# The first quad's first row half of an expert layer, multiplied expert by expert with its row blocks in four column groups and folded afterwards

## The chip, the cores and the metric

One core of one Trainium2 chip. The metric is the time of one execution on the device, in microseconds (us). A core has five engines with queues of their own: TensorE (PE; its weight loads are PEld), VectorE (DVE), ScalarE (ACT), GpSimd (POOL) and SyncE (SP), which here only issues transfers; 16 DMA engines carry the transfers. SBUF is the on-chip memory, PSUM the accumulators of TensorE (eight banks of 128 x 512 fp32).

## What is computed

A decoder trunk of two layers on 256 tokens of width 1024, all in fp32. Layer 0 is a gated linear recurrence, layer 1 block-sparse attention; each is followed by a hierarchical mixture of 32 experts, which is what the change touches:

```python
def hier_moe(h, w_group, b_group, w_expert, b_expert, w_in, w_out):
    # top-1 group of 4, top-2 experts of the 8 in it, weights of each token
    ...
    def expert_block(args):
        xb, e = args
        hu = xb @ w_in[e]                                    # 1024 -> 2 x 512
        return (jax.nn.silu(hu[:, :EXPERT_FF]) * hu[:, EXPERT_FF:]) @ w_out[e]   # 512 -> 1024
    ...
```

Every expert's weights (4 MB for w_in, 2 MB for w_out) are read once per layer.

## The kernel before, in words

An expert layer goes through the 32 experts in 8 quads of 4 (QUADS, GRP). Each expert has room for 32 tokens (BLK), so a quad's tokens fill 128 rows. For a quad the tokens' features are gathered by products with a 0/1 matrix (`gather`, and for a layer's first quad `first_half` and `second_half`) into PSUM, scaled and copied to xgT, [128 features of block k, 4 experts x 32 tokens]. Then `up` multiplies: for a row block k of 128 rows of w_in, for the gate and for the up columns, four matmuls, one per expert, each with a stationary operand of 128x32 (the expert's tokens) and a moving one of 128x512 (the weights). The four write to different strips of 32 partitions of one bank, so they stand in the four column groups of the array. Eight row blocks make two row halves of four blocks each. Then come tanh (L699) and the products of silu (L1214, L1219), four transposes (`hidden_T`), `down` with w_out, and `combine`, which adds the result to the tokens' sums.

**Loads.** The weights come in slots of 2.097 MB (128 partitions x 16 KB): per quad, r = 12u to 12u+3 are the first row halves of its four experts, the next four the second row halves, the last four w_out. They go through a ring of 8 slots, all issued on the SP queue in a fixed order, each load waiting until the slot's last reader is done: `rows_done` (first row half of a quad multiplied), `up_done`, `down_done`. A layer's first loads are placed ahead of the layer; four of them (r = 0, 8, 9, 10) have homes outside the ring (EXTRA_HOME), r = 0 in the work regions 0 and 1.

**Around the change.** The loads r = 12, 13, 14 (first row halves of quad 1's experts) go to the slots of r = 1, 2, 3, which hold quad 0's first row halves of experts 1, 2, 3. Before, quad 0's first row half was multiplied block by block over all four experts. After block 0 and after block 1 TensorE signals `first_k_done`, and `load_freed` (L405 to L419, issue on L417) loads the same block, 0.5 MB, of the three new weights; after `rows_done` it loads blocks 2 and 3, 1 MB each: nine transfers. r = 15 to 18 (L372) wait for `up_done` of quad 0, r = 19 for its `down_done`, and r = 20 to 23 (w_out of quad 1) for `rows_done` and what follows in quad 1. DVE scales block 0 of the gathered tokens as soon as it is there (L965), blocks 1 to 3 after the gather (L967); ACT scales blocks 4 to 7 (`weighted_columns`, L638). Block 2's product stands behind half of the second gather, block 3's behind the other half. The counts per expert (two products with `ones`) follow, then the second row half (`up`, 64 records, since an fp32 matmul leaves two records) and the next quad's gather.

Of the kernel before, what the change touches and what calls it, by code (L numbers as in the profile page):

```python
# [15 lines left out]
ALU = mybir.AluOpType  # L16
# [3 lines left out]
P = 128  # L20
T = 256
TT = T // P
D = 1024
# [36 lines left out]
LATE = SMALL + 204 + 2 * KD * (NG + E) + NG + P  # L60
TAKEN = 1024
# [6 lines left out]
def build(nc, x, hg_w_in, hg_w_out, w_kv, att_w_q, att_w_o, rel_bias, moe_w_in, moe_w_out, c_turned, c_rows, c_first, c_late, c_masks, c_bucket, c_future, out):  # L68
    with ExitStack() as ctx:
# [14 lines left out]
        late = sb("late", [P, LATE])  # L84
# [16 lines left out]
        turn = late[:, LATE - P:LATE]  # L101
        ms = sb("ms", [P, 18])
# [60 lines left out]
        rt = region(5)  # L163
        wgt = rt[:, 384:448].rearrange("p (q a e) -> p q a e", a=TT, e=GRP)
# [52 lines left out]
        first_k_done = sem("first_row_blocks_done")  # L217
        first_k_gathered = sem("first_row_block_gathered")
        freed_in = [sem(f"freed_row_block{k}_in") for k in range(2)]
# [44 lines left out]
        def heads_bank(j, hp):  # L264

            return (4 + hp - 2) if j == 0 else (6 + hp) % 8

# [50 lines left out]
        def _(sp):  # L318
# [27 lines left out]
            def load_expert(layer, r, dst, src, it):  # L346
# [59 lines left out]
            def experts(layer):  # L406
                def load_freed(r0):
                    for part, ks in enumerate((slice(0, 1), slice(1, 2), slice(2, KD // 2))):
                        if part == 2:
                            sp.wait_ge(*expert_read(layer, 0, 0))  # L410
                        else:
                            sp.wait_ge(first_k_done, 2 * layer + part + 1)
                        for r in range(r0, r0 + GRP - 1):
                            c = ring_chunk(layer, r, 0)

                            def copy(dst, src):
                                sp.dma_start(dst[:, ks, :], src[:, ks, :])\  # L417
                                  .then_inc(loaded[c % RING] if part == 2 else freed_in[part], 16)

                            expert_chunk(layer, r % QC // GRP, GRP * (r // QC) + r % GRP, copy, chunk(c))  # L420

                def load_next(r, it):
                    if freed(r, it):
                        if r == RING + EXTRAS:
                            load_freed(r)
                        return
# [126 lines left out]
        def _(act):  # L553
# [107 lines left out]
            def moe(layer):  # L661
# [45 lines left out]

                act.wait_ge(gat_done, 2 * P0 + 2)
# [1316 lines left out]
```

## Time and profile before

| | |
|---|---|
| median of 3 runs | 1167.86 us (1167.62 to 1168.41) |
| the profiled execution | 1167.82 us, span 1166.0 us |
| TensorE busy | 866.5 us (74%) |
| VectorE, ScalarE, GpSimd busy | 269.6, 132.5, 24.0 us |
| moved | 447.76 MB, mean 384 GB/s |
| mean granted TensorE clock | 0.875 |

The page cuts the span into 40 slices of 29 us. In the lines of slices a digit is the busy share in tenths, and PEclk is the granted clock of TensorE in tenths of full speed. Slices 1 to 5 are the mixer of layer 0, 6 to 20 its experts, 21 to 25 the mixer of layer 1, the rest its experts. Times in the trace count from the start of the span.

### The profile page before, as it was taken

To read this page: it belongs to the slowest core of one execution; us is meant where nothing else is said; L and a number is where in the kernel's file an instruction comes from. 1 tells how busy PE (TensorE), PEld (TensorE's weight loads), DVE (VectorE), ACT (ScalarE), POOL (GpSimd) and SP (SyncE) were. 2 spreads that over 40 slices of the span, in tenths; PEclk is the share of its full clock that TensorE was granted. 3 is DMA by queue.
4 is the path that set the end of the run, shared out by engine and by line. 5 is a ranking of instruction groups with operands and counts; after the bars stand their busy time and mean duration, and the time that the engine had idled before them with its cause. 6 is when DMAs were issued, how large, how long until landed. Compare 5 with 4: busy or idle time off the path is not lost.

```text
span 1166.0 us, 12503 instructions
## 1 busy us (share of the span) xinstructions
PE 866.5 (74%) x5238; PEld 412.6 (35%) x5238; DVE 269.6 (23%) x504; ACT 132.5 (11%) x328; POOL 24.0 (2%) x27
## 2 busy tenths in 40 slices
PE   9999999946566655656689999986565656565666
PEld 7965655312121212222234565532222222222222
DVE  3565673010101010101038746301010101010102
ACT  2011211100000000000011241110000000000000
POOL 1000110000000000000002100000000000000000
PEclk9999999977878787878899999998788887877789
DMA  9985588999999999999999937899999999999997
GB/s 351 281 323 211 216 319 329 422 428 428 429 427 428 430 427 428 428 427 429 415 410 405 377 145 286 317 428 427 429 426 428 428 428 429 427 428 427 427 420 294
DMA packets 51817, 447.76 MB, mean 384 GB/s; under 512 B 4496, under 2 KB 6840, under 8 KB 26936
## 3 DMA queue, kind: packets, MB, share of 16 engines
q1 hardware_dynamic: 49696, 444.43, 92.1%
q10 hardware_dynamic: 2072, 2.62, 1.2%
q8 instruction: 38, 0.62, 0.2%
q14 instruction: 11, 0.09, 0.0%
HBM read 444.41 MB, written 2.62 MB: 383 GB/s over the span
## 4 chain that ended last, share of the span: by engine, by line
DMA 45%; PE 45%; SPq 5%; issue 2%; DVE 1%; ACT 1%; POOL 0%; DVEq 0%; POOLq 0%
PE ps L1394 44%; DMA ring<-in_moe_w_in 29%; DMA ring<-in_moe_w_out 15%; SPq L466 3%; SPq L372 2%; DMA ring<-in_w_kv 1%; PE ps L1397 1%; DMA xs<-const_turned 0%; ACT ps L668 0%; DVE work L1141 0%; ACT work L638 0%; DVE work L1274 0%; SPq L500 0%; DVE work L1225 0%; ACT work L664 0%
## 5 line engine op out<-in xcount | busy, mean ns | idle before, releaser
L1394 PE MATMUL ps<-ring,work 128*32 128x512 f32 (+1 forms) x3360 | 602.6, 694 | 272.4 <-DMA ring<-in_moe_w_in 149.0
L1394 PEld LDWEIGHTS ps<-ring,work 128*32 128x32 f32 (+1 forms) x3360 | 190.8, 135 | 621.7 <-issue 605.0
L1214 DVE SCALAR_TENSOR_TENSOR work<-work,ps 128x512 f32<-128x512 f32 x16 | 11.0, 688 | 678.5 <-ACT work L699 678.5
L1394 PE MATMUL ps<-work 128*128 128x128 f32 (+4 forms) x498 | 127.5, 437 | 3.0 <-ACT work L706 1.6
L1394 PEld LDWEIGHTS ps<-work 128*128 128x128 f32 (+2 forms) x498 | 64.1, 176 | 62.1 <-issue 59.1
L638 ACT ACTIVATE work<-ps,first 128x128 f32<-128x128 f32 x120 | 34.3, 369 | 272.0 <-PE ps L1394 272.0
L1394 PEld LDWEIGHTS ps<-work,xs 128*128 128x128 f32 x512 | 58.8, 192 | 15.1 <-issue 15.1
L1394 PE MATMUL ps<-work,xs 128*128 128x128 f32 x512 | 62.8, 279 | 0.0
L706 ACT COPY work<-ps 128x512 f32<-128x512 f32 x32 | 18.8, 586 | 316.2 <-PE ps L1394 316.2
L1394 PE MATMUL ps<-work,ring 128*128 128x128 f32 (+1 forms) x352 | 53.3, 313 | 0.3 <-DVE work L817 0.3
L1394 PEld LDWEIGHTS ps<-work,ring 128*128 128x128 f32 x352 | 49.3, 191 | 4.5 <-issue 0.6
L1397 PE MATMUL ps<-first,work 128*128 128x128 f32 x160 | 21.8, 276 | 17.7 <-DVE work L1219 15.1
L699 ACT ACTIVATE work<-ps 128x512 f32<-128x512 f32 x16 | 9.6, 597 | 198.3 <-PE ps L1394 198.3
L1397 PEld LDWEIGHTS ps<-first,work 128*128 128x128 f32 x160 | 17.6, 140 | 30.6 <-issue 19.0
L524 POOL TENSOR_TENSOR rstd<-ms,mhalf 128x1 f32<-128x1 f32 (+2 forms) x12 | 15.6, 1309 | 614.2 <-DVE ms L802 614.2
L1219 DVE SCALAR_TENSOR_TENSOR work<-work,ps 128x512 f32<-128x512 f32 x16 | 16.5, 1033 | 32.6 <-PE ps L1394 32.6
L1084 DVE TENSOR_TENSOR work<-work 128x512 f32<-128x512 f32 x28 | 17.5, 686 | 22.0 <-PE ps L1394 22.0
L1394 PE MATMUL ps<-ones 128*128 128x128 f32 x158 | 21.7, 296 | 1.0 <-POOL mhalf L517 1.0
L1394 PEld LDWEIGHTS ps<-ones 128*128 128x128 f32 x158 | 20.2, 208 | 4.6 <-issue 3.6
L1225 DVE COPY work<-ps 128x512 f32<-128x512 f32 x16 | 11.1, 691 | 23.0 <-PE ps L1397 23.0
L1394 PE MATMUL ps<-spare,work 128*32 128x512 f32 x32 | 15.8, 652 | 0.0
L598 ACT COPY work<-work 128x512 f32<-128x512 f32 x14 | 8.2, 631 | 41.9 <-DVE work L1084 22.7
(155 smaller groups left out, 347.8 us busy)
## 6 DMA issues: line engine op xcount, KB each, us to landing
ring<-in_moe_w_in SPq DMA_DIRECT2D x112, 2048.0 KB, 20.0
ring<-in_moe_w_out SPq DMA_DIRECT2D x50, 2048.0 KB, 19.6
ring<-in_moe_w_in SPq DMA_DIRECT2D x22, 1024.0 KB, 16.4
ring<-in_hg_w_in SPq DMA_DIRECT2D x7, 2048.0 KB, 20.3
ring<-in_moe_w_out SPq DMA_DIRECT2D x24, 512.0 KB, 14.3
work<-in_moe_w_out SPq DMA_DIRECT2D x4, 2048.0 KB, 9.9
ring<-in_moe_w_in SPq DMA_DIRECT2D x12, 512.0 KB, 7.4
ring<-in_w_kv SPq DMA_DIRECT2D x3, 2048.0 KB, 24.9
```

The source lines that it names most:

```text
L372: sp.dma_start(dst, src).then_inc(loaded[c % RING], 16)
L466: sp.dma_start(down_view(chunk(c))[:, k:k + 1, cs], down_rows(moe_w_out[layer, E - GRP + x])[:, k:k + 1, cs])\
L524: pool.tensor_tensor(rstd[:, c0:c1], ms[:, c0:c1], mhalf[:, c0:c1], ALU.pow).then_inc(rstd_ready, 1)
L638: i = act.activation(xgT[:, buf, 4 * half + k, :], ps[:, bank, k * P:(k + 1) * P], ACT.Copy, scale=wrow[:, layer, 4 * half + k:4 * half + ...
L699: act.activation(en, ps[:, 6, :], ACT.Tanh, scale=0.5).then_inc(exp_done, 1)
L706: act.copy(y[:, half * 512:(half + 1) * 512], ps[:, 6 + half, :]).then_inc(y_ready, 1)
L1084: return dve.tensor_tensor(part, part, tv[:, :, a, :, 1 - block].unsqueeze(3) .to_broadcast([P, H, nb, m]), ALU.mult)
L1214: dve.scalar_tensor_tensor(en, en, 1.0, ps[:, 6, :], ALU.add, ALU.mult).then_inc(silu_ready, 1)
L1219: dve.scalar_tensor_tensor(hid_rows, en.rearrange("p (q k) -> p q k", k=KF), 0.5, ps[:, 7, :].rearrange("p (q k) -> p q k", k=KF), ALU.mul ...
L1225: dve.tensor_copy(hidT, ps[:, 5, :].rearrange("p (k s) -> p k s", s=P)).then_inc(hidT_ready, 1)
L1394: return pe.matmul(o, l, r, start=start, stop=stop)
L1397: return pe.transpose(o, i, ident)
```

## The change

The first row half of a layer's first quad is multiplied expert by expert, in the order 1, 0, 2, 3 (OPENING). For one expert the four row blocks k go to the four column groups: strip k of a bank gets the expert's tokens times block k alone. ACT copies the gate bank and DVE the up bank to SBUF (`halves`), and at the end a product with `fold` (four 32x32 identities one above the other, 128x32) adds the four strips and puts them where `up` would have them. The slots of experts 1, 2 and 3 are refilled by one whole load each, after the first, third and fourth expert (`opened`). The scaling of the first four gathered blocks is dealt out anew (DVE 0 and 1 together and 3, ACT 2), and all three must be done before the first product.

```diff
+OPENING = (1, 0, 2, 3)
...
+        halves = [region(0)[:, 0:D], region(5)[:, 896:1920], region(0)[:, D:2 * D], region(1)[:, 0:D]]
...
+        def part_bank(n):
+            return 2 + 2 * (n % 3)
...
+                elif freed(r, it):
+                    sp.wait_ge(opened, GRP * layer + OPENING.index(r - RING - EXTRAS + 1) + 1)
...
-                def load_freed(r0):
-                    for part, ks in enumerate((slice(0, 1), slice(1, 2), slice(2, KD // 2))):
...
+                def gate_part_copy(n):
+                    x = OPENING[n]
+                    act.wait_ge(opened, GRP * layer + n + 1)
+                    act.copy(halves[x][:, 0:FF], ps[:, part_bank(n), :]).then_inc(gate_part, 1)
+
+                act.wait_ge(gat_done, 2 * P0 + 1)
+                act.activation(xgT[:, 0, 2, :], ps[:, 4, 0:P], ACT.Copy, scale=wrow[:, layer, 2:3]).then_inc(first_rows, 1)
+                gate_part_copy(0)
+                gate_part_copy(1)
                 act.wait_ge(gat_done, 2 * P0 + 2)
                 weighted_columns(layer, 0, 1, 1).then_inc(xg_ready, 2)
+                gate_part_copy(2)
+                gate_part_copy(3)
...
                 dve.wait_ge(first_k_gathered, layer + 1)
-                dve.tensor_scalar(xgT[:, 0, 0, :], ps[:, 2, 0:P], wrow[:, layer, 0:1], None, ALU.mult).then_inc(first_rows, 1)
+                dve.tensor_tensor(xgT[:, 0, 0:2, :], ps[:, 2:4, 0:P],
+                                  wrow[:, layer, 0:2].unsqueeze(2).to_broadcast([P, 2, P]), ALU.mult)\
+                   .then_inc(first_rows, 1)
                 dve.wait_ge(gat_done, 2 * layer * QUADS + 1)
-                dve.tensor_tensor(xgT[:, 0, 1:4, :], ps[:, 3:6, 0:P],
...
+                dve.tensor_scalar(xgT[:, 0, 3, :], ps[:, 5, 0:P], wrow[:, layer, 3:4], None, ALU.mult).then_inc(first_rows, 1)
...
                 gate_weights(layer)
+                for n, x in enumerate(OPENING):
+                    dve.wait_ge(opened, GRP * layer + n + 1)
+                    dve.tensor_copy(halves[x][:, FF:D], ps[:, part_bank(n) + 1, :]).then_inc(up_part, 1)
                 passes(layer)
+                dve.wait_ge(rows_done, P0 + 1)
...
+                        def opening(n):
+                            x, bank = OPENING[n], part_bank(n)
+                            chunk_in(x)
+                            for gate_up in range(2):
+                                for k in range(KD // 2):
+                                    i = mm(ps[k * BLK:(k + 1) * BLK, bank + gate_up, :], xgT[:, 0, k, x * BLK:(x + 1) * BLK],
+                                           rows_view(home(layer, x, it))[:, k, gate_up * FF:(gate_up + 1) * FF])
+                            i.then_inc(opened, 1)
+
+                        def folded(gate_up):
+                            for x in range(GRP):
+                                i = mm(ps[x * BLK:(x + 1) * BLK, 6 + gate_up, :], fold,
+                                       halves[x][:, gate_up * FF:(gate_up + 1) * FF], True, False)
+                            return i
...
-                            for k in range(KD // 2):
-                                if k < 2:
-                                    pe.wait_ge(first_rows, 2 * layer + k + 1)
-                                else:
-                                    second_half(range(2 * k - 4, 2 * k - 2))
...
+                            pe.wait_ge(first_rows, 3 * (layer + 1))
+                            opening(0)
+                            opening(1)
+                            second_half(range(0, 2))
+                            opening(2)
+                            second_half(range(2, 4))
+                            pe.wait_ge(gate_part, GRP * layer + 1)
+                            pe.wait_ge(up_part, GRP * layer + 1)
+                            opening(3)
                             mm(ps[:, 0, 0:E], ones[:], asg[:, 0, :], True, False)
                             mm(ps[:, 0, 0:E], ones[:], asg[:, 1, :], False, True).then_inc(count_done, 1)
+                            pe.wait_ge(gate_part, GRP * (layer + 1))
+                            pe.wait_ge(up_part, GRP * (layer + 1))
+                            for gate_up in range(2):
+                                i = folded(gate_up)
+                            i.then_inc(rows_done, 1)
```

The first gather also signals blocks 0 and 1 together (before, block 0 alone), and `late`, a constant loaded in layer 0's mixer, grows by the 32 columns of `fold`.

## Rows read from the trace of the kernel before

**Rows 1.** the page: transfer rate in 40 slices, and the chain that ended last

```profile
GB/s 351 281 323 211 216 319 329 422 428 428 429 427 428 430 427 428 428 427 429 415 410 405 377 145 286 317 428 427 429 426 428 428 428 429 427 428 427 427 420 294
...
DMA 45%; PE 45%; SPq 5%; issue 2%; DVE 1%; ACT 1%; POOL 0%; DVEq 0%; POOLq 0%
```

**Rows 2.** windows: length, busy PE, PEld, DVE, ACT, POOL, PEclk, DMA share, GB/s

```profile
250.00:530.00 280.00, 174.71 (x1168) 64.30 (x1160) 16.63 (x30) 20.29 (x55) 0.00 (x0) 0.80 1.01 428
```

**Rows 3.** windows of both layers' starts, same columns

```profile
178.00:182.00 4.00, 4.00 (x41) 2.08 (x43) 2.67 (x13) 0.26 (x1) 0.00 (x0) 1.00 0.01 4
182.00:189.00 7.00, 7.00 (x63) 3.05 (x55) 0.00 (x0) 1.15 (x4) 0.00 (x0) 1.00 0.92 276
189.00:199.36 10.36, 10.36 (x95) 5.29 (x95) 3.95 (x15) 1.56 (x5) 0.00 (x0) 1.00 1.03 422
199.36:223.83 24.47, 22.67 (x165) 8.65 (x164) 2.20 (x5) 2.50 (x7) 0.00 (x0) 0.93 1.02 429
739.00:746.00 7.00, 7.00 (x63) 3.05 (x51) 0.00 (x0) 1.14 (x4) 0.00 (x0) 1.00 0.94 274
746.00:756.19 10.19, 10.19 (x94) 5.12 (x94) 3.96 (x15) 1.41 (x5) 0.00 (x0) 1.00 1.04 431
756.19:780.66 24.47, 22.67 (x179) 10.00 (x178) 2.20 (x5) 3.78 (x12) 0.00 (x0) 1.00 1.01 428
```

**Rows 4.** timeline of SP's queue: start, length, line, operation, count

```profile
181.28 9.20 SPq L417 DMA_DIRECT2D ring<-in_moe_w_in  x9
196.44 15.54 SPq L372 DMA_DIRECT2D ring<-in_moe_w_in  x5
222.29 2.77 SPq L372 DMA_DIRECT2D ring<-in_moe_w_out  x4
...
738.24 8.90 SPq L417 DMA_DIRECT2D ring<-in_moe_w_in  x9
753.42 13.84 SPq L372 DMA_DIRECT2D ring<-in_moe_w_in  x5
777.57 1.75 SPq L372 DMA_DIRECT2D ring<-in_moe_w_out  x4
```

**Rows 5.** one load alone: its issue, and windows behind it

```profile
165.51 0.33 SPq L372 DMA_DIRECT2D ring<-in_moe_w_in  x1
...
166.00:168.00 2.00, 2.00 (x16) 1.62 (x14) 1.93 (x4) 0.49 (x1) 0.22 (x1) 1.00 0.83 180
168.00:170.00 2.00, 2.00 (x8) 1.11 (x8) 1.31 (x8) 0.00 (x0) 0.00 (x0) 1.00 0.99 426
```

**Rows 6.** timeline of PE, layer 0: first set, last set, counts, second half

```profile
179.30 0.63 PE L1394 MATMUL ps<-ring,work 128*32 128x512 f32 x3
...
188.21 0.61 PE L1394 MATMUL ps<-ring,work 128*32 128x512 f32 x3
188.75 0.63 PE L1394 MATMUL ps<-work,ones 128*128 128x32 f32 x4
189.31 7.07 PE L1394 MATMUL ps<-ring,work 128*32 128x512 f32 x64
```

**Rows 7.** scalings (timeline of layer 0); copies of 128x512 (by line)

```profile
178.73 0.35 DVE L965 TENSOR_SCALAR work<-ps,first 128x128 f32<-128x128 f32 x1
...
179.40 0.56 DVE L967 TENSOR_TENSOR work<-ps,first 128x384 f32<-128x384 f32 x1 [0.32 <-PE ps L1394]
...
187.00 1.15 ACT L638 ACTIVATE work<-ps,first 128x128 f32<-128x128 f32 x4 [8.13 <-PE ps L1394]
...
L1225 DVE COPY work<-ps x16: 690/692/692, 202.1 to 1146.3; 128x512 f32<-128x512 f32 x16
...
L706 ACT COPY work<-ps x32: 586/586/587, 208.2 to 1159.7; 128x512 f32<-128x512 f32 x32
```

**Rows 8.** a pause of PE, and the window behind it (PEclk: granted clock)

```profile
201.38 0.87 PE L1397 MATMUL ps<-first,work 128*128 128x128 f32 x6 [1.23 <-ACT work L638]
...
203.00:207.00 4.00, 4.00 (x24) 1.00 (x20) 1.28 (x4) 0.00 (x0) 0.00 (x0) 0.57 1.00 422
```

More of the change, by code:

```diff
@@ L83, in build @@
         first = sb("first", [P, FIRST])
-        late = sb("late", [P, LATE])
+        late = sb("late", [P, LATE + BLK])
         ident = first[:, 0:P]
@@ L101, in build @@
         turn = late[:, LATE - P:LATE]
+        fold = late[:, LATE:LATE + BLK]
         ms = sb("ms", [P, 18])
@@ L216, in build @@
         first_pick, first_rows = sem("first_quad_tile0_picked"), sem("first_quad_half_gathered")
-        first_k_done = sem("first_row_blocks_done")
+        opened = sem("first_quad_expert_half_read")
         first_k_gathered = sem("first_row_block_gathered")
-        freed_in = [sem(f"freed_row_block{k}_in") for k in range(2)]
+        gate_part, up_part = sem("first_quad_gate_parts_copied"), sem("first_quad_up_parts_copied")
         asg_ready, pos_done, nblk_ready = sem("assigned"), sem("positions_done"), sem("blocks_ready")
@@ L406, in experts @@
             def experts(layer):
-                def load_freed(r0):
-                    for part, ks in enumerate((slice(0, 1), slice(1, 2), slice(2, KD // 2))):
-                        if part == 2:
-                            sp.wait_ge(*expert_read(layer, 0, 0))
-                        else:
[L412 to L420, printed above, removed]
                 def load_next(r, it):
[L423 to L426, printed above, removed]
                     expert_chunk(layer, r % QC // GRP, it * (GRP * UN) + (GRP * (r // QC) + r % GRP),
@@ L1724, in moe @@
                 pe.wait_ge(pick_ready, P0 + 1)
-                first_half(1, [0]).then_inc(first_k_gathered, 1)
-                first_half(1, range(1, 4)).then_inc(gat_done, 1)
+                first_half(1, [0, 1]).then_inc(first_k_gathered, 1)
+                first_half(1, [2, 3]).then_inc(gat_done, 1)
                 def combine(it, u, a, half, start, stop):
@@ L1742, in body, with chunk_in @@
                         n0 = type(it) is int and it * UN + q < 1
+                        def chunk_in(r):
+                            if in_extra(r, it):
+                                pe.wait_ge(extra_in[EXTRA_HOME[r]], 16 * (layer + 1))
+                            else:
+                                arrived(ring_chunk(layer, r, it), it)
                         def group_in(r):
                             for x in range(GRP):
-                                if in_extra(r + x, it):
-                                    pe.wait_ge(extra_in[EXTRA_HOME[r + x]], 16 * (layer + 1))
-                                else:
-                                    if freed(r + x, it):
-                                        for row_block in freed_in:
-                                            pe.wait_ge(row_block, 16 * (GRP - 1) * (layer + 1))
-                                    arrived(ring_chunk(layer, r + x, it), it)
+                                chunk_in(r + x)
+                        def opening(n):
[11 more added lines that the diff above has]
+                            return i
                         def group(r):
@@ L1990, in constants @@
         + [spread(v[n][l]) for l in range(2) for n in ("moe_b_group", "moe_b_expert")] + router
-        + [spread(np.arange(NG, 0, -1) * 1e36), np.eye(P)[::-1]], axis=1)
+        + [spread(np.arange(NG, 0, -1) * 1e36), np.eye(P)[::-1], np.tile(np.eye(BLK), (GRP, 1))], axis=1)
     first, late = (np.ascontiguousarray(a, dtype=np.float32) for a in (first, late))
```

12 lines of the change are left out of this document (1 added, 11 removed).

## The prediction

> **What bounds the kernel now.** I read the page's forty slices first. The transfers run at 427 to 430 GB/s through most of both expert layers; the mixer stages and the start of each expert layer fall far below that, and the chain that ended last is DMA 45%, PE 45% [rows 1]. Over 250 to 530 us the core moves 428 GB/s while TensorE is busy 175 of 280 us [rows 2]. So once an expert layer is under way the transfers are the bound, without a gap, and nothing lost there can be made up: the end of the layer moves by exactly what the stream of loads is late when it becomes continuous. The question is when that is, before and after.
>
> The stream's position I count in slots of 2.097 MB from the first freed slot on (loads r = 12, 13, 14, then 15 and on). Layer 0: nothing moves from 178 to 182 us; the nine pieces of L417 bring 276 GB/s for 7 us (1.93 MB by 189); then 422 GB/s, so three slots (6.29 MB) have passed at 199.36 and eight (16.78 MB) at 223.83 [rows 3]. Layer 1: 274 GB/s from 739 to 746, three slots at 756.19, eight at 780.66 [rows 3].
>
> The SP queue's own rows then show what each load waited for [rows 4]. First pieces go out at 181.28, r = 15 to 18 at 196.44 (when TensorE has finished quad 0's second row half), r = 20 to 23 at 222.29 (quad 1's first row half done). How long from issue to bytes: the lone load at 165.51 has moved 180 GB/s x 2 us = 0.36 MB by 168, 0.85 us at 426 GB/s, so its bytes began at 167.15, 1.64 us after the issue [rows 5]. So r = 15 could flow from 198.1, 1.3 us before the stream was free (no gap), while r = 20 could flow from 223.93, just as the eighth slot ended at 223.83: layer 0's stream is held there by TensorE and by itself at once. In layer 1, r = 20 (issued 777.57) could flow at 779.2, 1.5 us early. The whole stage has little slack in TensorE.
>
> **The change part by part.**
> Removed: nine issues of 0.5 or 1 MB per layer, with their low rate. Added: three whole loads, released after one, three and four experts have been multiplied.
>
> Start of the products. Before, the first set of four started at 179.30, right behind the gather [rows 6], since block 0's scaling (0.35 us from 178.73) was done; now all four blocks must be scaled. Blocks 2 and 3 can be scaled only when the gather ends, about 179.4 (L967 started at 179.40); a 128x128 scaling takes 0.35 us on DVE, and on ACT four take 1.15 together, so one about as long as on DVE [rows 7]. The first product starts near 179.87: **0.58 us late**. The bounds are 0.4 and 0.8.
>
> The products themselves. The same 32 matmuls, four at a time in the four column groups. A set (four records; an fp32 matmul leaves two) takes 7.07/16 = 0.44 us [rows 6]; one expert is four sets, 1.75. The two pieces of the other gather and the changes of shape stay, so 179.30 to 188.75 (9.45 us) stays. Whether four column groups read four slots or one slot, and whether four partial sums go to one bank's strips, no row tells; as every set has the same shapes I take no difference.
>
> Evacuation. Eight copies of 128x512: 0.586 us on ACT (L706), 0.69 on DVE (L1225) [rows 7]. Three pairs lie beside the next expert's 1.75 us and are hidden; were that cover gone they would cost 0.69 each. The last pair is not: the last set ends at 188.81 + 0.58 = 189.39, DVE's copy at about 190.15, the fold can start at 190.2; the count products fill 0.56 us of that, up to 189.89. Cost **0.31 us**. The Trainium skill (TensorEngine Tiling (Array Packing), PSUM Bottleneck) says that column tiling does not speed the emptying of PSUM, whose copies may become the limit. By the rows above a copy takes 0.4 of a product, so here only the last would show; by the rule taken whole, three more pairs would, another 2.1 us.
>
> The fold. Eight matmuls 128x32 by 128x512, four column groups again: four sets, **1.75 us**. The upper bound is sixteen records one after another, 7 us; below 1.7 the nearest rows give nothing, so 1.4 at the least. I take 1.75, as the shape equals that of [rows 6].
>
> Sum: TensorE starts quad 0's second row half at 191.9 in place of 189.31, **d = 2.6 us** (2.0 to 3.4).
>
> Waits behind these. On ACT the scaling of the second four blocks stands behind two copies; they end before its gather does (about 187.5). On DVE the passes count moves to 190.2 to 191.3 and is needed at 211; the next picks stand behind the wait for the fold, ready about 193.4, needed by a gather at 199. The late load grows by 16 KB (0.04 us at 428 GB/s), long before anything reads it; POOL's queue is not touched. On SP the first load is released at 181.28 + 0.58 = 181.87, and nothing else stands behind it but the loads in question.
>
> The stream after, layer 0. Bytes from 181.87 + 1.64 = 183.5. The second load is released at about 186.5 (bytes 188.1, the first lasts to 188.4), the third at 189.5, so the three run together: 14.7 us at 428 GB/s, done at 198.2, **1.2 us earlier** than 199.36. That is the gain. But r = 15 goes out at 196.44 + 2.6 and flows at 200.7: a gap of 2.5 us, and the stream is 1.3 us later than before. Eight slots are through at 225.2, and r = 20 goes out at 222.29 + 2.6, flows at 226.5, against 223.9: **layer 0 loses 2.6 us**. Layer 1: three slots done at 738.24 + 0.59 + 1.64 + 14.7 = 755.2, r = 15 flows at 753.42 + 2.6 + 1.64 = 757.7, against 756.19: 1.5 us late; r = 20 could flow at 781.8, the stream is free at 782.1. **Layer 1 loses 1.5 us.** Sum +4.1 us on the profiled execution's 1167.82 us (span 1166.0); the median shown is 1167.86, so no correction: **1171.9 us**.
>
> **The rivals.** A change under 0.2% (2.3 us) can't be told from none by a measurement of this kernel; that bound is used below.
> A, forecast: +4.1, with d from 2.0 to 3.4 it is +2.8 to +5.8. Chance 0.44.
> B, the clock no longer falls in layer 0. From 203 to 207 us the granted clock is 0.57, after pauses of TensorE (1.23 us before 201.38) [rows 8]; that costs 4 x 0.43 = 1.7 us of the path to 222.29. Layer 1, with the same work, has 1.00 from 756 to 781 where layer 0 has 0.93 from 199 to 224 [rows 3]. If the shift of 2.6 us makes it go away, r = 20 flows at 224.8, the stream decides (225.2), +1.3 and +1.5: 1170.6. Chance 0.16.
> C, d is half what I say (the sets of one expert faster, or the fold's), 1.3 us: layer 0 +1.3 at r = 20, layer 1 756.4 against 756.19, +0.2: 1169.3, no change. Chance 0.20. For it: all sum terms come from shapes of before, none from the fold itself. Against: the records of such sets are very even.
> D, the other side: whole refills win. The mechanism is the earlier end of the three slots, at 198.2; the place is the issue of r = 15; it decides if TensorE is done with quad 0 by 198.2 - 1.64 = 196.6, that is d under 0.2 us. Then layer 0 gains 1.2, layer 1 1.0: 1165.6. A gain beyond that needs bytes sooner than 1.64 us after the issue; 0.3 us of that per layer would give 1165.0. Chance 0.11, most of it counted as faster.
> E, worse: the clock falls in the new pauses (at 179.4 and 189.9) and the second row half runs slow, 1.7 us in each layer: +4.3 and +3.2, 1175.3. B's rows show a fall towards the lower level, 1.2 GHz, behind a pause of 1.23 us; the new ones are 0.5 and 0.3 us, shorter. The Trainium skill (TensorE: Matmul & The Clock Gate, Part 1) says that the low clock is the default and that activity releases it; by that rule, and the trace agrees in layer 0 and not in layer 1, pauses bring it back. Or the fold's sets do not overlap (+5.2 us of d: about 1182), or evacuation sets the pace (d = 4.7: 1176). Chance of all 0.09.
> That the change doesn't do what it says: if the second or third load missed its turn, the stream would have 2.5 us to spare before r = 15, so this costs nothing and is in A.
>
> **How the numbers follow.** The likeliest is A, 1171.9. Slower by over 0.2% (above 1170.2): A less a little at its lower edge (0.42), two thirds of B (0.11), E (0.09): 0.62. Within: C, the rest of A and B, a part of D: 0.29. Faster: 0.09. The range goes from C's lower part, 1168.7, to A's upper bound and a little of E, 1173.8.
>
> **What would show it.** Right: the slot loads' first issue near 181.9 and 400 GB/s or more from 184 on; a hole in the transfers of some 2 us around 199 and around 756; r = 15 issued 2 to 3 us later than before; four sets of the fold in some 1.75 us after a pause of 0.3; 428 GB/s from 250 to 530 us unchanged. Wrong: no hole at 199 (d is small), or the second row half starting before 190.5, or the loads' rate under 400 GB/s with whole slots. A granted clock under 1.0 between 180 and 199 would be E, and 1.0 throughout 203 to 210 would be B.

## The result, and the profile after

| | before | after |
|---|---|---|
| median of 13 runs each | 1167.86 us (1166.83 to 1169.59) | 1170.19 us (1169.22 to 1173.6) |
| ratio of after to before | | 1.0024, 95% interval 1.0017 to 1.0032 |
| the profiled execution | 1167.82 us, span 1166.0 | 1170.03 us, span 1168.2 |
| nine of the runs after | | 1169.22 to 1170.36 |
| the other four | | 1171.9, 1172.65, 1173.21, 1173.6 |

The change makes the kernel slower by 0.24%. That is what was forecast in its sign and in most of its mechanism; the size is that of case B (1170.6) and not of the likeliest case A (1171.9).

Both layers start 0.30 us earlier in the profiled execution after (the load r = 11 went out at 170.82 instead of 171.12). But for the 16 KB that `late` has grown by, all of the change lies behind that issue, and in the profiles of the experiments below, with and without the change, it stands anywhere from 170.5 to 172.5 us, so I don't put it down to the change. So I give times below also as counted from that issue, in layer 1 from 728.06 (before) and 728.98 (after).

First the page after: the transfer rate in 40 slices, and the chain that ended last, as in [rows 1].

```profile
GB/s 348 280 326 209 216 326 308 430 426 428 429 428 426 429 427 429 429 427 426 417 411 404 371 144 289 298 427 427 430 426 428 427 428 429 427 430 425 429 418 296
...
PE 45%; DMA 45%; SPq 5%; issue 2%; DVE 1%; ACT 1%; POOL 0%; DVEq 0%; POOLq 0%
```

The seventh slice (175 to 204 us) moves 308 GB/s against 329, the 23rd to 26th, with layer 1's start, 371, 144, 289, 298 against 377, 145, 286, 317. The rest is the same stream at the same rate. So the loss is where the forecast looked for it.

Now the path of TensorE at layer 0's start: the timeline of PE (start, length, line, operation, count), which answers to [rows 6].

```profile
179.52 1.92 PE L1398 MATMUL ps<-ring,work 128*32 128x512 f32 x16 [0.46 <-ACT work L703]
181.26 1.90 PE L1398 MATMUL ps<-work 128*32 128x512 f32 x16
...
187.12 1.92 PE L1398 MATMUL ps<-ring,work 128*32 128x512 f32 x16
188.97 0.63 PE L1398 MATMUL ps<-work,ones 128*128 128x32 f32 x4
189.95 1.93 PE L1398 MATMUL ps<-work,late 128*32 128x512 f32 x16 [0.34 <-DVE work L1255]
191.66 7.08 PE L1398 MATMUL ps<-ring,work 128*32 128x512 f32 x64
```

Read the starts. An expert takes 1.74 us (179.52 to 181.26). From the first product to the counts it is 188.97 - 179.52 = 9.45 us, to the hundredth what it was. The fold takes 191.66 - 189.95 = 1.71 us behind a pause of 0.34 for DVE's copy. The second row half starts at 191.66 + 0.30 = 191.96 against 189.31: **d = 2.65 us**; 2.6 was forecast.

The copies that this waits for, in the timeline of ACT and DVE; the first pair stands beside a product, the last one does not.

```profile
181.51 0.58 ACT L700 COPY work<-ps 128x512 f32<-128x512 f32 x1 [2.04 <-PE ps L1398]
181.58 0.69 DVE L1255 COPY work<-ps 128x512 f32<-128x512 f32 x1 [0.73 <-PE ps L1398]
...
189.11 0.58 ACT L700 COPY work<-ps 128x512 f32<-128x512 f32 x1 [0.27 <-PE ps L1398]
189.11 0.69 DVE L1255 COPY work<-ps 128x512 f32<-128x512 f32 x1 [2.25 <-PE ps L1398]
```

The SP queue after, which answers to [rows 4] (the first row covers r = 12 to 19; a narrower window gives r = 15 to 18 alone, the second row).

```profile
181.50 31.14 SPq L380 DMA_DIRECT2D ring<-in_moe_w_in  x8
...
198.79 2.05 SPq L380 DMA_DIRECT2D ring<-in_moe_w_in  x4
...
222.95 1.75 SPq L380 DMA_DIRECT2D ring<-in_moe_w_out  x4
...
739.66 31.14 SPq L380 DMA_DIRECT2D ring<-in_moe_w_in  x8
...
756.95 2.10 SPq L380 DMA_DIRECT2D ring<-in_moe_w_in  x4
...
781.11 1.76 SPq L380 DMA_DIRECT2D ring<-in_moe_w_out  x4
```

r = 15 goes out 198.79 + 0.30 - 196.44 = 2.65 us later, all of d. And the transfers, in windows (length, busy of the engines, granted clock, DMA share, GB/s), against [rows 3]:

```profile
182.00:189.00 7.00, 7.00 (x61) 2.93 (x53) 1.65 (x3) 2.30 (x7) 0.00 (x0) 1.00 0.99 346
184.00:189.00 5.00, 5.00 (x44) 1.89 (x42) 0.69 (x1) 1.62 (x5) 0.00 (x0) 1.00 1.01 413
189.00:198.00 9.00, 8.66 (x84) 3.51 (x84) 3.58 (x15) 1.18 (x2) 0.00 (x0) 1.00 0.98 410
198.00:202.00 4.00, 4.00 (x37) 3.33 (x30) 1.06 (x1) 1.14 (x4) 0.00 (x0) 1.00 0.65 205
203.00:207.00 4.00, 2.69 (x26) 1.26 (x30) 2.20 (x5) 0.69 (x3) 0.00 (x0) 1.00 1.03 442
756.00:760.00 4.00, 4.00 (x39) 3.17 (x29) 1.05 (x1) 1.08 (x4) 0.00 (x0) 1.00 0.63 188
```

The whole loads do come faster (346 GB/s from 182 to 189 against 276, and 413 once they run, from 184 on). Then the hole: 205 GB/s from 198 to 202 is (428 - 205) x 4 / 428 = 2.1 us without transfers, and 188 in layer 1 is 2.2 us. And the granted clock from 203 to 207 is 1.00, where it was 0.57 [rows 8]. From 250 to 530 us the rate is 428 GB/s as before.

### The profile page after: what moved, and what is told of

It reads as the page before. It is cut to its first block, busy times and chain, and to the rows that moved or that the text cites. A ratio compares the mean times of both kernels' runs of the same rounds, so it can differ in the third digit from the quotient of the medians.

```text
span 1168.2 us, 12569 instructions
## 1 busy us (share of the span) xinstructions
PE 868.8 (74%) x5270; PEld 413.4 (35%) x5270; DVE 274.9 (24%) x512; ACT 137.5 (12%) x338; POOL 24.0 (2%) x27
## 4 chain that ended last, share of the span: by engine, by line
PE 45%; DMA 45%; SPq 5%; issue 2%; DVE 1%; ACT 1%; POOL 0%; DVEq 0%; POOLq 0%
PE ps L1398 45%; DMA ring<-in_moe_w_in 28%; DMA ring<-in_moe_w_out 14%; SPq L455 3%; SPq L380 2%; DMA ring<-in_w_kv 2%; PE ps L1401 1%; DMA ring<-in_hg_w_in 1%; ACT ps L657 0%; DVE work L1141 0%; ACT work L627 0%; DVE work L1278 0%; SPq L489 0%; DVE work L1255 0%; DVE work L1225 0%
## 5 line engine op out<-in xcount | busy, mean ns | idle before, releaser
L1398 PE MATMUL ps<-work 128*128 128x128 f32 (+4 forms) x498 | 114.7, 429 | 3.0 <-ACT work L695 1.6
```

The lines of the kernel that those rows point to most:

```text
L1398: return pe.matmul(o, l, r, start=start, stop=stop)
```

## The experiments

Each kernel was compared with the kernel before on the same chip. The last columns come from its profiled execution, all counted from the issue of r = 11 in each layer: start of quad 0's second row half, issue of r = 20, the moment at which eight slots had passed (the GB/s of windows of 1 us, added up to 16.78 MB), and the length of the layer from there (layer 0 to layer 1's r = 11, layer 1 to the end of the span). "Late" is the difference of that length to the kernel before. Where two numbers stand they are layer 0 / layer 1.

| kernel | median, us over before (interval of the ratio) | second half | r = 20 | eight slots | late |
|---|---|---|---|---|---|
| before | 0 | 18.19 / 18.22 | 51.17 / 49.51 | 52.70 / 52.55 | 0 (556.94 / 437.94) |
| after | +2.33 (1.0017 to 1.0032) | 20.84 / 20.84 | 52.13 / 52.13 | 54.14 / 54.06 | 1.22 / 1.28 |
| 1 no fold | +1.4 (0.9979 to 1.0027) | 19.01 / 19.01 | 52.00 / 50.30 | 52.57 / 53.38 | 0.60 / 2.46 |
| 2 fold twice | +6.1 (1.0040 to 1.0069) | 22.56 / 22.56 | 53.84 / 53.84 | 55.86 / 55.83 | 2.92 / 2.91 |
| 3 fold late | +2.4 (1.0010 to 1.0030) | 19.01 / 19.02 | 52.01 / 53.72 | 53.19 / 53.78 | 1.05 / 3.40 |
| 4 cut loads | +3.4 (1.0023 to 1.0052) | 20.84 / 20.84 | 52.12 / 52.13 | 54.18 / 54.09 | 2.61 / 1.28 |
| 5 delay 1.2 | +3.5 (1.0021 to 1.0047) | 19.38 / 19.42 | 50.66 / 52.40 | 52.91 / 53.43 | -0.08 / 0.98 |
| 6 delay 2.5 | +3.2 (1.0019 to 1.0043) | 20.73 / 20.77 | 52.02 / 52.06 | 53.94 / 54.06 | 0.83 / 1.25 |
| 7 delay 4.8 | +6.4 (1.0042 to 1.0068) | 22.96 / 23.00 | 54.24 / 54.28 | 56.17 / 56.30 | 3.36 / 3.52 |
| 8 whole, late | +11.3 (1.0084 to 1.0113) | 18.18 / 18.22 | 49.47 / 49.50 | 58.46 / 58.73 | 5.46 / 5.79 |
| 9 pieces, late | +14.9 (1.0113 to 1.0144) | 18.19 / 18.22 | 50.42 / 50.67 | 60.17 / 60.27 | 7.42 / 8.91 |
| 10 after, filled | +2.5 (1.0012 to 1.0031) | 20.84 / 20.84 | 52.13 / 52.13 | 54.03 / 54.18 | 1.02 / 1.37 |
| 11 before, filled | -0.25 (0.9988 to 1.0006) | 18.18 / 18.23 | 49.47 / 49.51 | 52.63 / 52.64 | -0.16 / 0.87 |
| 12 after again | +3.0 (1.0016 to 1.0036) | 20.83 / 20.84 | 52.12 / 52.12 | 54.11 / 54.28 | 1.14 / 2.38 |

Is what the stream has lost by the eighth slot ever made up? Counting the bytes on in the same way, the changed kernel is 1.21, 1.26 and 1.23 us behind the kernel before when 40, 100 and 199 MB have passed in layer 0, and 1.34, 1.44 and 1.36 us at 40, 100 and 175 MB in layer 1. It is not, in any of these kernels: each keeps its distance within 0.3 us from 40 MB to the last loads of an expert layer. Where "late" is well above that distance, the difference arises outside the stretch that the change touches: in kernel 4 (layer 0: 1.5 to 1.6 us late up to 201 MB, the other 1.1 us only in the mixer of layer 1 behind it) and, in layer 1, at the very end of kernels 1, 3, 9, 11 and 12.

### The delay alone: 5, 6, 7

Idle products between the row halves of the kernel before, nothing else (5, 11 or 21 of them):

```diff
                             mm(ps[:, 0, 0:E], ones[:], asg[:, 1, :], False, True).then_inc(count_done, 1)
+                            keep_busy(11, 2)
```

> The kernel before with five idle products (128x128 by 128x128, 1.24 us) between the first and the second row half of the first quad, in each layer. Theory 1: r = 15 flows at 199.34 against 199.36, so nothing is lost there; r = 20 costs 1.3 us in layer 0 only where the clock falls there; layer 1 +0.1. So 0.1 to 1.4 us over the kernel before. Rival (delay is hidden): 0. Rival (all of the delay is paid in each layer, no slack): +2.5.

> The kernel before with eleven such products, 2.7 us in each layer, about the delay that the change brings (2.65), and nothing else of the change. Theory 1: layer 0 +1.5 (+2.8 with a fall of the clock), layer 1 +1.6: 3.1 to 4.4 us over the kernel before, hardly more than the changed kernel, since the earlier end of the three whole loads is worth nothing once r = 15 comes late. A hole near 200 us, shorter than the changed kernel's. Rival (whole loads or copies are to blame): 0.

> The same with 21 products, 5.2 us in each layer. Theory 1: beyond the slack of 1.2 us in each layer the delay is paid in full: +8.0 (+9.3 with a fall of the clock in layer 0), ratio 1.007 to 1.008. Rival (delay hidden): 0.

Measured: the second row half is 1.2, 2.5 and 4.8 us late. Take 6 first. With TensorE about as late as in the changed kernel it has the changed kernel's loss: eight slots 1.24 / 1.51 us late (after: 1.44 / 1.51), 3.2 us in the median against 2.3 to 3.0. Its SP queue and the hole behind it:

```profile
198.50 2.34 SPq L372 DMA_DIRECT2D ring<-in_moe_w_in  x4
```

```profile
197.00:199.00 2.00, 2.00 (x21) 0.86 (x14) 0.41 (x1) 0.00 (x0) 0.00 (x0) 1.00 0.96 406
199.00:201.00 2.00, 2.00 (x20) 2.00 (x20) 0.65 (x1) 0.54 (x3) 0.00 (x0) 1.00 0.87 221
```

The hole is shorter than the changed kernel's, because its three slots end later; the end of the hole is the same. Kernel 7 continues the line: 4.8 us of delay, eight slots 3.47 / 3.75 late. So behind a slack of 1.3 us in layer 0 and 1.0 in layer 1 the delay is paid one for one, whether the slots are filled in pieces or whole. "The delay is hidden" falls. In the median kernel 7 is a miss: +6.4 where +8.0 was expected, and 1.007 lies outside the interval. Most of that is the delay itself, 4.8 us and not 5.2; with 4.8 the same sum gives 7.2, which the interval (4.9 to 7.9 us) holds.

The three profiled executions fit theory 1 (5: eight slots 0.2 / 0.9 late, layers -0.08 / 0.98). Of the 0.9 of kernel 5, 0.4 stand at the third slot already; the rest comes where the granted clock falls behind quad 0, in layer 1: r = 20 goes out at 52.40 (50.66 in layer 0, which has no fall), and the rate is down to 336 GB/s from 780 to 784 us, while the eighth slot passes. The median of 5 does not: +3.5 where 0.1 to 1.4 was expected. Its five runs are 1169.32, 1169.55, 1171.31, 1173.29 and 1173.51 us, and the profile belongs to the 1169.55. What adds 2 to 4 us to the others no profile shows; what is known of it comes below.

### The price of the fold: 1, 2, 3

Kernel 1 leaves the fold out (so the first quad's first row half is missing from the result in both layers), 2 makes it twice, 3 puts it behind the second row half and releases r = 15 to 18 before it (with it, and not shown, the first expert's copies wait for the second expert, one of the copies has another home, and DVE's wait for `rows_done` is gone):

```diff
 # 1
-                            pe.wait_ge(gate_part, GRP * (layer + 1))
-                            pe.wait_ge(up_part, GRP * (layer + 1))
-                            for gate_up in range(2):
-                                i = folded(gate_up)
-                            i.then_inc(rows_done, 1)
+                            pe.wait_ge(gate_part, GRP * layer + 3)
+                            pe.wait_ge(up_part, GRP * layer + 3)
+                            mm(ps[:, 4, 384:512], ones[:], ones[:]).then_inc(rows_done, 1)
 # 2
-                            for gate_up in range(2):
-                                i = folded(gate_up)
+                            for again in (True, False):
+                                for gate_up in range(2):
+                                    i = folded(gate_up, again)
 # 3, behind the waits and the product of 1
+                        if first:
+                            for gate_up in range(2):
+                                i = up(group(r), 1, 0, gate_up, range(KD // 2), True)
+                            i.then_inc(lb_in, 1)
+                            pe.wait_ge(gate_part, GRP * (layer + 1))
+                            pe.wait_ge(up_part, GRP * (layer + 1))
+                            folded(0).then_inc(up_done, 1)
+                            folded(1).then_inc(up_done, 1)
...
+                elif is_int(it, 0) and r < RING + EXTRAS + 2 * GRP - 1:
+                    sp.wait_ge(lb_in, layer + 2)
```

> The changed kernel without the product with fold and without the wait for the last pair of copies; all copies are still made. So the first quad's first row half is left out of the result in both layers. Theory 1 (TensorE's delay decides, through the issues of r = 15 and r = 20): the second row half starts some 0.6 us later than in the kernel before instead of 2.65, the three whole loads are done before r = 15 can flow, and both layers gain: 0 to 1.4 us under the kernel before (ratio 0.999 to 1.000), 2.3 us or more under the changed kernel; no hole of transfers near 199 and 757 us. Rival (the loss comes with the whole loads or the copies, not with the delay): it stays 2 us above the kernel before.

> The changed kernel with the fold made twice (the same result), 1.75 us more of TensorE in each layer. Theory 1: each layer is later by all of it, since r = 15 already comes late: 3.5 us over the changed kernel, 5.8 to 7 us over the kernel before (ratio 1.005 to 1.006), and the hole of transfers near 199 us grows from 2 to about 4 us. Rival (TensorE waits 10 us for loads later anyway, its delay is hidden): as the changed kernel, +2.3 us.

> The changed kernel with the fold moved behind the second row half, and r = 15 to 18 released when that half has been read, before the fold (the same result). Only the later start of the products is ahead of r = 15; the path to r = 20 still carries start and fold, 2.3 us. Theory 1: no hole near 199 us; r = 20 then decides: +0.6 us in layer 0 without a fall of the clock there (+2.3 with one), +0.85 in layer 1, so 1.4 us over the kernel before (up to 3), about 0.9 us under the changed kernel. A variant of theory 1 in which only r = 15 counts: 1.4 us under the kernel before. Rival (whole loads or copies are to blame): as the changed kernel.

Kernel 2 came as expected: TensorE 1.72 us later, eight slots another 1.72 / 1.77, the median 3.1 to 3.8 us over the changed kernel's. Its hole (same columns as above):

```profile
197.00:199.00 2.00, 2.00 (x24) 0.79 (x20) 0.69 (x1) 0.45 (x1) 0.00 (x0) 1.00 0.46 197
199.00:203.00 4.00, 4.00 (x37) 3.01 (x30) 1.05 (x1) 0.76 (x3) 0.00 (x0) 1.00 0.47 115
```

2 x (1 - 197/428) + 4 x (1 - 115/428) = 4.0 us, the 4 expected. With kernel 6 this is the firmest result here: more delay of TensorE alone, by the fold or by idle products, brings the same loss.

Kernel 1 recovers part of the loss and not all of it: +1.4 us where 0 or less was expected. Its interval holds no change, and it also overlaps that of the changed kernel, so the times alone settle nothing, and the profile has to speak. Layer 0 has a fall of the clock behind quad 0, as the kernel before has. So r = 20 goes out at 52.00 (50.30 in layer 1, which has none), 0.83 us later than in the kernel before, and the rate sinks there:

```profile
203.00:207.00 4.00, 3.81 (x21) 0.95 (x25) 1.65 (x5) 0.00 (x0) 0.00 (x0) 0.59 1.01 434
222.00:226.00 4.00, 4.00 (x39) 3.48 (x32) 0.00 (x0) 1.14 (x4) 0.00 (x0) 1.00 0.90 311
```

That is the forecast's second gate: eight slots are 0.13 early, and layer 0 ends 0.60 late. In layer 1 eight slots are 0.83 late, though r = 15 is only 0.8 us late there and had 1.0 us of slack. Layer 1's windows:

```profile
752.00:755.00 3.00, 3.00 (x31) 1.26 (x24) 0.82 (x2) 0.00 (x0) 0.00 (x0) 1.00 1.02 431
755.00:756.00 1.00, 1.00 (x12) 1.00 (x11) 0.47 (x1) 0.00 (x0) 0.00 (x0) 1.00 1.23 360
756.00:760.00 4.00, 2.77 (x25) 2.50 (x23) 0.02 (x1) 2.29 (x8) 0.00 (x0) 1.00 0.85 287
```

r = 15 was issued at 754.35, so its bytes could flow at 756.0; 287 GB/s over the next four is 1.3 us lost. By the working of the forecast the queue was dry for 0.5 us only. So the gain of an early end of the three slots goes into a slow restart. Layer 0 has it too, smaller (352 GB/s from 197.66 to 201.66, 0.7 us), and so has kernel 3, whose r = 15 stands at the same place (371 GB/s from 196 to 202, 0.8 us). Why it costs more here than where the gap is wide (the changed kernel, 2, 6 and 7 lose their nominal gap within 0.3 us) stays open.

Kernel 3 was a miss in the median: +2.4 us, as the changed kernel, where 1.4 was expected. Its profile shows the second gate. Layer 0: no delay at r = 15 beyond 0.8 us, and eight slots 0.5 us late, but r = 20 at 52.01, and the layer is 1.05 late: the forecast's second gate, since the fold is still ahead of r = 20. Layer 1 had a fall of the clock in this execution:

```profile
764.00:768.00 4.00, 4.00 (x32) 1.05 (x26) 0.31 (x1) 0.00 (x0) 0.00 (x0) 0.65 0.98 416
780.00:784.00 4.00, 4.00 (x37) 2.34 (x30) 0.00 (x0) 0.00 (x0) 0.00 (x0) 1.00 0.73 225
```

```profile
782.18 1.95 SPq L382 DMA_DIRECT2D ring<-in_moe_w_out  x4
```

r = 20 goes out at 53.72 instead of 52.01 after the issue of r = 11, 1.7 us later; the stream is short of loads from 780 to 784, and from there to 175 MB it is 2.5 us late, where layer 0 is 1.0. So the fall of 1.7 us cost 1.5. This is the mechanism of the forecast's case A, seen in a neighbouring kernel: once TensorE is late, a fall of the clock behind quad 0 is paid almost in full. The other 0.9 us of the 3.40 arise at the end of the layer, where this execution has no fall of the clock; they are not explained.

### What whole slots are worth: 4, 8, 9

Kernel 4 is the changed kernel with each whole load cut in four; 8 is the kernel before without `load_freed` (three whole loads after `rows_done`); 9 is the kernel before with its nine pieces, all after `rows_done`:

```diff
 # 4
+                        sp.wait_ge(opened, GRP * layer + OPENING.index(r - RING - EXTRAS + 1) + 1)
+                        def pieces(dst, src):
+                            for k in range(KD // 2):
+                                sp.dma_start(dst[:, k:k + 1, :], src[:, k:k + 1, :])\
...
 # 8
-                    if freed(r, it):
-                        if r == RING + EXTRAS:
-                            load_freed(r)
-                        return
 # 9
-                        if part == 2:
-                            sp.wait_ge(*expert_read(layer, 0, 0))
-                        else:
-                            sp.wait_ge(first_k_done, 2 * layer + part + 1)
+                        if not part:
+                            sp.wait_ge(*expert_read(layer, 0, 0))
```

> The changed kernel with each of the three whole loads cut in four loads of one row block, 0.5 MB, released at the same moments. It measures what the whole slots are worth. If the low rate of 276 GB/s before was due to the size of the pieces (theory 1), three slots take 22.8 instead of 14.7 us, and each layer is some 5 us later than in the changed kernel: about 12 us over the kernel before (ratio 1.010). Rival (the low rate came from too few bytes released): 400 GB/s or more, as the changed kernel.

> The kernel before with r = 12, 13 and 14 loaded whole, but only after the whole first row half (rows_done), so with no early release. Theory 1: bytes flow from 190.5, three slots at 205.2 instead of 199.36, +5.9 us in each layer, 11.9 us over the kernel before (ratio 1.010). This is what an early release is worth against none; if the stream's position is not what decides, it would be under +3.

> The kernel before with the same nine pieces in the same order, but all of them released only after the whole first row half, when TensorE no longer reads the slots they go to. It asks why the pieces came at 233 to 311 GB/s before while pieces of the same size came at 340 to 414 in the run with cut loads. Theory P: writing into a slot while TensorE reads its other blocks is what slows them; then they come at 400 GB/s from 191 us on and the run is within 1.5 us of the run with whole late loads (ratio about 1.010). Theory Q: the order over three slots, each piece 4 KB of every 16 KB, slows them; then 250 to 300 GB/s for the first six, some 4 us more in each layer, ratio about 1.017.

Kernel 8 came as expected (eight slots 5.8 / 6.2 late, the median 11.3 against 11.9): the position of the stream is what decides, and an early release is worth that much against none.

Kernel 4 was a miss, and a useful one. Its pieces come at 378 GB/s once they run (whole loads: 413), three slots pass some 0.8 us later than in the changed kernel, and eight slots pass at 54.18 / 54.09, as in the changed kernel, since r = 15 comes later still:

```profile
182.00:184.00 2.00, 2.00 (x23) 1.04 (x15) 0.77 (x2) 0.59 (x1) 0.00 (x0) 1.00 0.70 174
184.00:189.00 5.00, 5.00 (x43) 2.01 (x43) 0.77 (x2) 1.70 (x6) 0.00 (x0) 1.00 1.03 378
```

So it isn't the size of a piece that made the low rate of [rows 3]. (That its median is +3.4 is not the pieces' doing as far as the profile shows: the 1.1 us extra of layer 0 arise in the mixer behind it.) Kernel 9 asks further. TensorE no longer reads the slots, yet:

```profile
191.00:192.00 1.00, 1.00 (x13) 0.27 (x9) 0.90 (x11) 0.00 (x0) 0.00 (x0) 1.00 0.62 193
192.00:197.00 5.00, 5.00 (x52) 1.55 (x48) 1.85 (x4) 0.60 (x1) 0.00 (x0) 1.00 0.98 268
197.00:203.00 6.00, 4.77 (x42) 3.89 (x35) 1.06 (x1) 2.29 (x8) 0.00 (x0) 1.00 1.02 418
```

268 GB/s at a DMA share of 0.98: the engines are busy and move little. Theory P falls. Q is right about the rate and wrong about how long: the slow part is 0.19 + 5 x 0.268 = 1.5 MB, which is the first block of the three experts and no more; the second block comes at full rate. The same 1.5 MB is slow in the kernel before (from 182 to 188). Eight slots are 1.7 / 1.5 us later than in kernel 8, where the 4 us of Q were expected. What makes just the first block of three slots slow stays open.

### The clock: 10, 11, 12

Idle products in TensorE's two pauses behind quad 0, in the changed kernel (10) and in the one before (11); 12 is the changed kernel once more.

```diff
+                        if first:
+                            keep_busy(4, 2)
                         if not last:
                             pe.wait_ge(xg_ready, it * (2 * UN) + (2 * q + 4))
...
+                        if first:
+                            keep_busy(2, 2)
                         pe.wait_ge(hidT_ready, it * UN + (q + 1))
```

> The changed kernel with idle products (four and two) in TensorE's two pauses of 1.23 and 0.57 us behind the first quad, in both layers. Theory C (the runs of the changed kernel split in a group at 1169.2 to 1170.4 and one at 1171.9 to 1173.6 since the granted clock falls behind these pauses in some): no fall between 200 and 210 us or 758 and 770, median 1170.0 and no run over 1171.5. Rival (falls at the end of a layer or others make the upper group): the upper group stays.

> The kernel before with the same idle products. The clock no longer falls from 203 to 207 us, so r = 20 goes out 1.7 us earlier in layer 0. Theory 1: the stream itself is free only at 223.8, so that is worth at most 0.4 us: 1167.5 to 1168.0 (ratio 1.000). Rival (the path of TensorE alone decides): 1.7 us less, 1166.2 (ratio 0.9985).

> The changed kernel once more, for its spread of times beside the filled one on the same chip, and for a second profile: about one run in three between 1171.5 and 1174. If the profile has a fall of the clock from 205 to 210 us, r = 20 goes out 1.7 us later than in the first profile and layer 0 is 1 us or more later, as the forecast's first case had it.

Kernel 11 decides a point of the forecast. The fall of [rows 8] is gone:

```profile
202.00:206.00 4.00, 3.88 (x39) 1.29 (x41) 1.87 (x5) 0.00 (x0) 0.00 (x0) 1.00 0.97 410
```

r = 20 goes out at 49.47 instead of 51.17, and the time is the same (-0.25 us, 0.9988 to 1.0006): the stream was not free before 52.6 anyway. In the kernel before, a fall of the clock behind quad 0 costs 0.3 us at the most (the stream of kernel 11 is that much earlier in layer 0), less than the medians can show.

Kernel 10 has 11 runs from 1169.17 to 1170.86 us, none above. Of the 22 runs of the changed kernel (13 and the 9 of kernel 12) six lie at 1171.78 or more. That agrees with the view that the upper group are runs with a fall in these pauses, and kernel 3's profile shows the mechanism. But it is not shown. Neither profile of the changed kernel caught a fall (both have 1.00 from 203 to 207 us), and if there were no difference, 0 of 11 against 6 of 22 would still come by luck one time in fifteen. Of all profiles with these pauses unfilled, the fall stands in four layers: the first of the kernel before and of kernel 1, the second of kernels 3 and 5. The changed kernel, 2, 4, 6, 7 and 12, all with 2.5 us of delay or more, have it in none of their twelve. What makes the upper group is open.

Nor are these pauses the only place. Kernel 12 is within 0.2 us of the first profile of the changed kernel up to the eighth slot and 1.1 us later at the end of layer 1 (2.38 against 1.28). The last products of `down` and what follows stand on the path there, and the granted clock differs. The windows of the layer's end, for the changed kernel, then for kernel 12, and for kernel 1, which lost 2.46 us in layer 1:

```profile
1153.00:1155.50 2.50, 0.34 (x5) 0.16 (x8) 0.00 (x0) 0.00 (x0) 0.00 (x0) 1.00 1.04 388
1155.50:1158.00 2.50, 1.76 (x20) 0.42 (x16) 0.00 (x0) 0.00 (x0) 0.00 (x0) 1.00 0.82 303
1158.00:1162.00 4.00, 3.20 (x19) 0.75 (x12) 1.08 (x1) 0.74 (x2) 0.00 (x0) 1.00 0.12 46
```

```profile
1155.50:1158.00 2.50, 2.25 (x20) 0.46 (x16) 0.00 (x0) 0.00 (x0) 0.00 (x0) 0.68 0.78 289
1158.00:1162.00 4.00, 3.20 (x18) 0.45 (x10) 0.41 (x1) 0.58 (x1) 0.00 (x0) 0.78 0.12 47
```

```profile
1155.50:1158.00 2.50, 2.46 (x16) 0.33 (x12) 0.00 (x0) 0.00 (x0) 0.00 (x0) 0.60 0.44 168
1158.00:1162.00 4.00, 3.20 (x18) 0.45 (x10) 0.82 (x1) 0.59 (x1) 0.00 (x0) 0.82 0.04 16
```

Granted 0.68 and 0.60 in place of 1.00, behind a pause in which TensorE waits for the last loads (2.46 us in kernel 12, 2.51 in kernel 1; 2.15 in the changed kernel). Kernel 11, built on the kernel before, has such a fall too, behind 3.21 us:

```profile
1153.00:1155.50 2.50, 2.50 (x16) 0.54 (x12) 0.00 (x0) 0.00 (x0) 0.00 (x0) 0.50 0.69 259
```

It is 0.87 us late in layer 1 for that (0.1 us at 175 MB), and its profiled run has 1168.07 us against its median of 1167.36. So this fall, worth 0.7 to 0.9 us, comes in some executions of either kernel (four of the fourteen profiles: 1, 9, 11 and 12); it spreads the times and does not tell the two kernels apart. Of kernel 1's 2.46 us it accounts for 0.8 and the slow restart for 0.8. The remaining 0.8 lie between the stream at 175 MB and the products behind the last loads, as in kernel 3, and stay unexplained.

## Why the prediction was right, and where it was off

**d.** 0.58 us for the later start, 0.31 for the last copies, 1.75 for the fold, 2.6 in all. Measured 0.22 + 0.30 = 0.52, (189.95 - 188.97) - (189.31 - 188.75) = 0.42, and 1.71: 2.65. The step held, including the choice not to charge the copies that lie beside products; by the rule of the Trainium skill (TensorEngine Tiling (Array Packing), PSUM Bottleneck) taken whole they would have cost 2.1 us more. They did not: the first pair ran beside the next product and only the last showed (0.34 us of pause, 0.42 in all). Column groups fed from one slot and fed from four run alike (1.74 us for four sets), which no row before could tell.

**r = 15, the first gate.** Forecast 2.6 us late, a hole of 2.5 us and 1.3 / 1.5 us lost behind it. Measured 2.65, holes of 2.1 and 2.2 us, eight slots 1.44 / 1.51 late. Right, and kernels 6, 7 and 2 show that it is cause and not coincidence. What the gate does near its edge was not foreseen: kernel 1, 0.2 us inside the slack, lost 0.8 us in layer 1.

**The gain of whole slots.** Forecast: three slots done 1.2 us earlier. Measured in layer 0: 6.29 MB had passed at 28.18 after the issue of r = 11, against 28.24; nothing. The loads come at 346 and 410 GB/s and not at 428, with a start of one busy and one poor microsecond (262 and 98 GB/s). That start also corrects a reading of the forecast. "Its bytes began at 167.15, 1.64 us after the issue" is worked back from the full rate. The windows of the kernel before show bytes of that lone load sooner, and then a poor stretch:

```profile
166.00:167.00 1.00, 1.00 (x7) 0.62 (x5) 0.96 (x3) 0.49 (x1) 0.22 (x1) 1.00 1.21 229
167.00:168.00 1.00, 1.00 (x11) 1.00 (x10) 0.97 (x2) 0.00 (x0) 0.00 (x0) 1.00 0.44 131
```

The first bytes move about 1 us after the issue, and 1.64 us is what issue and slow start cost together, against full rate at once. As such a sum it holds for the changed kernel's first load as well (issued at 181.50, 0.36 MB by 184, so 1.65 us). The missing gain made no difference to the sum, as anything earlier than r = 15 is lost, but it is why case D had less behind it than its working gave it. The forecast put the low rate before down to the pieces as such; kernel 4 shows that pieces of the same size can do 378 GB/s.

**r = 20, the second gate, is the term that was mis-sized.** "Layer 0 loses 2.6 us" rested on r = 20 at 222.29 + 2.6. It went out at 222.95 (223.25 on the clock of before), only 0.96 us later, for the granted clock stayed at 1.00 from 203 to 207 and gave back the 1.7 us; layer 0 lost 1.22 instead of 2.6. That is case B, which had 0.16 where A had 0.44. I had taken a fall that one execution showed to be part of the path. Nine of thirteen runs lie at B's number and four at A's or above; whether those four are case A, no profile shows. So the total came out as a case that I had held unlikely, and not as the sum of A. Layer 1, where no fall was assumed, lost 1.28 against 1.5.

**The sum.** B: +1.3 and +1.5 gave 1170.6; the profiled execution has 1.22 + 1.28 - 0.30 (the earlier start) = 2.2 us, and its span grew by 2.2.

**The rivals.** C (d half as large) is out by the trace. D needed d under 0.2 us, which no kernel with the early whole loads has; in kernel 1, with d = 0.8, three slots end 0.7 us earlier than in the kernel before, and nothing of it is left at the eighth slot but 0.13 us in one layer. E: the fold's sets overlap, and no fall was seen between 180 and 199 us, in spite of the new pauses (0.46 and 0.34 us). The stretch of [rows 8] kept 1.00 in kernel 11, with its pauses filled, and also in both profiles of the changed kernel, with its pauses of 1.23 and 0.56 us unfilled. The Trainium skill's rule (TensorE: Matmul & The Clock Gate, Part 1), that activity releases the low clock, agrees with the first; the second shows that pauses like these do not bring the fall each time.

## What to carry to other kernels

When a stream of loads is the bound and only its start is ragged, count where the stream stands in bytes, before and after, and then look at each load whose issue waits for the engine you make slower: the earliest of them that comes after the queue is dry is the price, and an earlier end of what stands ahead of it is worth nothing. Here 2.65 us more on TensorE cost 1.2 to 1.5 us per layer, since the first gate had 1.0 to 1.3 us of slack. Don't price the last half microsecond before such a gate at nothing: kernel 1 lost 0.8 us there. A fall of the clock is nearly free while its stretch has slack (0.3 us at the most in the kernel before) and paid almost in full when it has none (1.5 of 1.7 us in kernel 3). That a change which eats the slack also widens the spread of the times would follow, but isn't shown: the changed kernel's runs spread over 4.4 us against 2.8 before, but the five each of kernels 2 and 7 only over 1.9 and 0.6. And one profile doesn't tell whether a fall of the clock belongs to a path: look at several executions before it goes into a sum.

## What the runs showed of the hardware that was not expected

The first block of three slots, in 0.5 MB pieces one per slot, came at 268 GB/s with the DMA engines 98% busy (kernel 9), while the four blocks of one slot in pieces of the same size came at 378 (kernel 4) and whole loads at 410 to 426 (the changed kernel, kernel 8). So the DMA busy share doesn't tell a slow stream from a fast one. A load issued on an idle queue has its first bytes about 1 us later and a poor microsecond behind them (229, then 131 GB/s). And a queue that is dry for a nominal 0.5 us lost 1.3 us in its restart (kernel 1), while nominal gaps of 1.0 us (kernel 6) to 3.6 us (kernel 2) cost no more than their length.
